# Gates of three sample tiles by accumulating indirect DMA instead of one-hot products, in a two-layer PEER trunk

## The chip, the cores and the metric

One core of a Trainium2 chip runs the whole program in one launch. The metric is device time in microseconds, 4672.34 us as the median of three runs before the change (4671.4 to 4675.66). The engines are named as the profile names them: PE is TensorE, DVE is VectorE, ACT is ScalarE, POOL is GpSimd and SP is SyncE, whose queue issues most of the plain DMAs.

## The reference, cut to what matters

Two layers run over 640 tokens: 128 prompt tokens and 512 sample tokens. Each layer ends with a PEER mixer. For each token and each of 8 heads it picks 16 of 16,384 experts by product keys, forms softmax gates, and sums gated expert outputs:

```python
s1 = einsum('thd,hnd->thn', q[:, :, 0], k1); s2 = einsum('thd,hnd->thn', q[:, :, 1], k2)
v1, i1 = top_k(s1, 16); v2, i2 = top_k(s2, 16)
cand = v1[..., :, None] + v2[..., None, :]          # 256 candidates per token and head
sv, si = top_k(cand, 16); eidx = i1 * 128 + i2 at si
gates = softmax(sv)
act = gelu(einsum('phkd,pd->phk', u_tab[eidx], x))  # one dot per chosen expert
out = einsum('phk,phkd->pd', gates * act, v_tab[eidx])
```

## The kernel before, in words

The kernel is a series of stages, each a block with one instruction stream per engine, joined by semaphores. The first layer's mixer is a gated DeltaNet (`delta_stage`), the second's a Fourier stage. Both layers then run PEER in two stages, under the names p0u/p0v and p1u/p1v.

The first expert stage (`experts_in_stage`, p0u and p1u) treats the two groups of tokens differently.

- **Sample tokens** are computed densely. A loop of 128 blocks `b` multiplies all 16,384 rows of the table `u` with all 512 sample tokens; a block has 128 experts and 24 products (L624). SP loads the block (`p0uraw`), ACT rounds it (`split_hi`, L651), DVE takes the rest (`split_lo`, L767), PE multiplies, ACT applies the gelu (L693) and stores to `a_scratch`. Only the routed gates make this sparse: a dense array `g_scratch[i1, i2, token]` holds each sample token's gate at its chosen experts and zero elsewhere, and the second stage multiplies both arrays.
- **Prompt tokens** are computed sparsely. For each of 128 slots (8 heads times 16 picks) POOL gathers one row of `u` per token by indirect DMA into `ring` (L757), and DVE takes the dot with the token (L872).

The gates are found tile by tile, 128 tokens each. PE makes the scores (L637), and DVE routes a tile in 21 steps (`route`): top 16 per key half, candidates, top 16 again, picks, gates. `route_plan` spreads these steps over blocks. In the kernel before, the prompt tile is the first (scores in block 1), and the four sample tiles follow.

For a sample tile, `g_scratch` is built from one-hot products, in 32 "quads" of 4 tokens: DVE compares the two key numbers of each pick with an iota (L778), ACT makes gated one-hots (L661 to L673), PE multiplies both per token (L612), ACT copies the sums to `g` (L681), and half a tile is stored in four DMAs (L686). `quad_plan` gives each sample tile a window of 23 blocks from block 32 on, `dot_plan` puts the prompt dots into blocks 32 to 127. Each engine works strictly in the order of this code, so a DVE wait in block `b` holds every later `split_lo`, and through it PE.

The second expert stage (`experts_out_stage`) reads `g_scratch` and `a_scratch` and multiplies with the table `v`; POOL gathers the prompt rows of `v` there.

Of the kernel before, what the change touches and what calls it, by code (L numbers as in the profile page):

```python
# [21 lines left out]
F32 = mybir.dt.float32  # L22
# [455 lines left out]
NQUADS = NQ * DEC_TILES  # L478
HALF_QUADS = NQ // 2
HALF_TOK = P // 2  # L480
STORES = 4
WIN = 23
W0 = 32
SCORES = [1, 15] + [W0 + WIN * k for k in range(DEC_TILES - 1)]
WINDOWS = [W0 + WIN * k for k in range(DEC_TILES)]
PAIRS = P
RING = 3


def quad_plan():  # L490

    plan = [[] for _ in range(P)]
    for k, w in enumerate(WINDOWS):
        for q in range(NQ):
            plan[w + q * WIN // NQ].append(k * NQ + q)
    return plan


def route_plan(n_tasks):

    plan = [[] for _ in range(P)]
    for k, s in enumerate(SCORES):
        span = (12, 11)[k] if k < 2 else WIN - 6
        for i in range(n_tasks):
            plan[s + 2 + i * span // n_tasks].append((k, i))
    return plan


def dot_plan():

    plan, n = [[] for _ in range(P)], 0
    for b in range(W0, P):
        for _ in range(2 if b >= P - (PAIRS - (P - W0)) else 1):
            plan[b].append(n)
            n += 1
    assert n == PAIRS, n
    return plan


def experts_in_stage(nc, m, tag, d, l, hi, lo, q_dram, a_dram, g_dram, x_dram, eidx, ew, eg):  # L520
# [10 lines left out]
        sm(x) for x in ("h_turned", "h_taken", "listed", "dot_done", "gelu_done", "weighed"))  # L531
    table = d[f"urows{l}"]
    with ExitStack() as es:
# [21 lines left out]
        tops = sb("tops", [P, 2, 4, P])  # L555
        oh1, oh2 = sb("oh1", [P, 3, QUAD, P]), sb("oh2", [P, 3, QUAD, P])
        g = [sb(f"g{j}", [P, P, HALF_TOK]) for j in range(2)]
# [9 lines left out]
        def _(sp):  # L567
# [12 lines left out]
            def load_q(k):  # L580
                if k:
                    sp.wait_ge(scored, k)
                else:
                    sp.wait_ge(spilled, 16)
                sp.dma_start(qt, q_dram[:, :, k * P:(k + 1) * P].rearrange("h p t -> p h t")).then_inc(q_full, 16)
# [5 lines left out]
            for b in range(2, P):  # L591
                load(b)
                for k in range(1, DEC_TILES + 1):
                    if b == SCORES[k - 1] + 6:
                        load_q(k)
                    if b == SCORES[k] - (0 if k < 3 else 3):
                        load_keys(k)

        @block.tensor
        def _(pe):  # L600
# [14 lines left out]
            for b in range(P):  # L615
# [11 lines left out]
                for k in range(DEC_TILES + 1):  # L627
                    if b == SCORES[k]:
# [3 lines left out]
                        if k > 1:  # L632
                            pe.wait_ge(t_taken, 2 * (k - 1))
# [5 lines left out]
                    if k and b == WINDOWS[k - 1] - 4:  # L639
                        pe.wait_ge(ready, k + 1)  # L640
# [5 lines left out]
        def _(act):  # L646
# [6 lines left out]
            def distances(n):  # L653
                if n < NQUADS and n % 2 == 0:
# [5 lines left out]
                    for e in range(QUAD):  # L660
                        last = nc.scalar.activation(oh2[:, n % 3, e, :], iota, ACT.Abs, bias=tops[:, k % 2, 0, t0 + e:t0 + e + 1], scale=-1.0)  # L661
                    last.then_inc(far, 1)

            def gated_one_hots(n):
                if n < NQUADS:
                    k, t0 = n // NQ, n % NQ * QUAD
                    act.wait_ge((far, near)[n % 2], n // 2 + 1)
                    for e in range(QUAD):
                        x, gate_t, minus_t = oh2[:, n % 3, e, :], tops[:, k % 2, 2, t0 + e:t0 + e + 1], tops[:, k % 2, 3, t0 + e:t0 + e + 1]
# [6 lines left out]
            def take(n):  # L676
                h, t0 = n // HALF_QUADS, n % HALF_QUADS * QUAD
                if n % HALF_QUADS == 0 and h >= 2:
# [4 lines left out]
            def store_half(h, s):  # L683
                i0, t0 = s * (P // STORES), h * HALF_TOK
                act.wait_ge(taken, (h + 1) * HALF_QUADS)
                act.dma_start(g_dram[i0:i0 + P // STORES, :, t0:t0 + HALF_TOK].rearrange("i p t -> p i t"),  # L686
# [18 lines left out]
            halves_due = []  # L705
            for b in range(P + 1):
# [19 lines left out]
                for k in range(DEC_TILES):  # L726
                    if b == WINDOWS[k] - 3:
                        act.wait_ge(turned, k + 1)
                        nc.scalar.copy(tops[:, k % 2, 0:3, :], bank[2][:, 0:3, :]).then_inc(t_taken, 1)
                        nc.scalar.mul(tops[:, k % 2, 3, :], bank[2][:, 2, :], -1.0).then_inc(t_taken, 1)  # L730
# [4 lines left out]
                for h, s in halves_due[:1]:  # L735
                    store_half(h, s)
                del halves_due[:1]
                for n in quads[b]:
# [3 lines left out]
                    if n % HALF_QUADS == HALF_QUADS - 1:  # L742
                        halves_due += [(n // HALF_QUADS, s) for s in range(STORES)]
            assert not halves_due
# [4 lines left out]
            act.wait_ge(g_stored, 16 * STORES * 2 * DEC_TILES)  # L749

        @block.gpsimd
        def _(pool):
            pool.wait_ge(listed, 1)
            for n in range(PAIRS):
                if n >= RING:
                    pool.wait_ge(dot_done, n - RING + 1)
                nc.gpsimd.indirect_dma_start(out=ring[:, n % RING, :], out_offset=None, in_=table,  # L757
                                             in_offset=bass.IndirectOffsetOnAxis(ap=eidx[:, n:n + 1], axis=0)).then_inc(row_full[n % RING], 16)

        @block.vector  # L760
        def _(dve):
# [7 lines left out]
            def plain_one_hots(n):  # L769
                if n < NQUADS:  # L770
# [6 lines left out]
                    for oh, row, sem in rows_of:  # L777
                        v.tensor_tensor(oh[:, n % 3], iota.unsqueeze(1).to_broadcast([P, QUAD, P]),  # L778
                                        tops[:, k % 2, row, t0:t0 + QUAD].unsqueeze(2).to_broadcast([P, QUAD, P]), ALU.is_equal).then_inc(sem, 1)
# [46 lines left out]
            def gates(k):  # L826
# [3 lines left out]
                out = gate[:] if k else eg[:].rearrange("p (h k) -> p h k", h=PEER_HEADS)  # L830
                v.tensor_tensor(out, ex[:], rden[:].unsqueeze(2).to_broadcast([P, PEER_HEADS, TOPK]), ALU.mult).then_inc(ready, 1)
                if k == 0:
                    v.scalar_tensor_tensor(out=eidx[:], in0=rows[:, 0, :], scalar=float(P), in1=rows[:, 1, :],
                                           op0=ALU.mult, op1=ALU.add).then_inc(listed, 1)

            def route(k, i):
                if i == 0:
                    dve.wait_ge(s_taken, 4 * (k + 1))
                    if k > 1:
# [1179 lines left out]
```

## Time and profile before

| | us |
|---|---|
| median of three runs | 4672.34 (4671.4 to 4675.66) |
| the profiled execution | 4669.94 |
| its span, first to last instruction | 4668.2 |
| DeltaNet stage | 338.8 to 681.9 |
| first expert stage, layer 0 (p0u) | 1000.7 to 1896.9 |
| second expert stage, layer 0 (p0v) | 1907.7 to 2617.1 |
| first expert stage, layer 1 (p1u) | 3016.7 to 3905.2 |
| second expert stage, layer 1 (p1v) | 3916.4 to 4627.8 |

PE is busy for 92% of the span, DVE for 69%, ACT for 38%, POOL for 31%. The four expert stages are two thirds of the span. A matmul's end is modelled in the profile, so the length of a block is read from the starts of its products and not from the busy time.

### The profile page before, as it was taken

Reading aid. Unit: us, or ns where it says so; the run is one execution under the profiler, and the core shown is the slowest. Engines: PE = TensorE matmul, PEld = TensorE weight load, DVE = VectorE, ACT = ScalarE, POOL = GpSimd, SP = SyncE. Lnnn points to the kernel's source line nnn. Section 1 sums busy time; section 2 is a strip of 40 time slices with the busy share of each in tenths; the row PEclk is TensorE's granted clock in tenths of the full one; section 3 lists DMA queues with packets and bytes.
Section 4 is the critical chain, followed back from the end, with each engine's and each line's share of the span. In section 5 each row is a group of like instructions: output and inputs, shape, how many; then the busy total and the mean of one; then the engine's idle time right before and its main releaser. Section 6 shows DMA issues by size and latency. Waiting matters only on the chain. (4 is left out here: it accounts for less than half of the span.)

```text
span 4668.2 us, 58501 instructions
## 1 busy us (share of the span) xinstructions
PE 4298.8 (92%) x21997; PEld 3603.2 (77%) x21997; DVE 3216.9 (69%) x5003; ACT 1785.2 (38%) x3370; POOL 1436.3 (31%) x844
## 2 busy tenths in 40 slices
PE   6988888899999999899999877999999997999997
PEld 1988886687888877688888476888888776888885
DVE  3658863338779876688888623187897865888886
ACT  1330002223667666222222232235777663222222
POOL 1001100100112123566777301000121234777763
PEclk9999988999999999999999988999999998999998
DMA  5210002344587788988888502455787889888884
GB/s 206 69 37 5 1 37 72 144 160 153 193 257 238 228 278 279 327 287 293 289 292 287 208 29 85 149 170 166 239 251 233 266 289 310 295 291 287 294 287 168
DMA packets 566628, 951.23 MB, mean 204 GB/s; under 512 B 295264, under 2 KB 317024, under 8 KB 560992
## 3 DMA queue, kind: packets, MB, share of 16 engines
q1 hardware_dynamic: 188000, 534.59, 33.5%
q0 software_dynamic: 73728, 268.47, 16.0%
q10 hardware_dynamic: 304640, 144.73, 10.6%
q8 instruction: 160, 2.62, 0.2%
q14 instruction: 100, 0.82, 0.0%
HBM read 794.56 MB, written 153.09 MB: 203 GB/s over the span
## 5 line engine op out<-in xcount | busy, mean ns | idle before, releaser
L757 POOL DMA_INDIRECT p1uring<-in_urows,p1eidx x128 | 171.7, 1342 | 851.0 <-DVE p1ew L872 608.2
L757 POOL DMA_INDIRECT p0uring<-in_urows,p0eidx x128 | 166.5, 1300 | 862.6 <-DVE p0ew L872 621.3
L624 PE MATMUL p0ups<-hi,p0uwhi 128*128 128x512 f32 x1024 | 419.0, 409 | 12.4 <-DVE p0uwlo L767 12.4
L624 PE MATMUL p1ups<-hi,p1uwhi 128*128 128x512 f32 x1024 | 417.0, 407 | 11.3 <-DVE p1uwlo L767 11.3
L986 PE MATMUL p1vps<-p1vwhi,p1vvhi 128*128 128x512 f32 x1024 | 399.2, 390 | 23.6 <-DVE p1vwlo L950 23.6
L986 PE MATMUL p0vps<-p0vwhi,p0vvhi 128*128 128x512 f32 x1024 | 399.4, 390 | 20.3 <-DVE p0vwlo L950 20.3
L624 PE MATMUL p0ups<-lo,p0uwhi 128*128 128x512 f32 x1024 | 404.8, 395 | 0.0
L624 PE MATMUL p0ups<-hi,p0uwlo 128*128 128x512 f32 x1024 | 404.4, 395 | 0.0
L624 PE MATMUL p1ups<-lo,p1uwhi 128*128 128x512 f32 x1024 | 402.9, 393 | 0.0
L624 PE MATMUL p1ups<-hi,p1uwlo 128*128 128x512 f32 x1024 | 402.6, 393 | 0.0
L986 PE MATMUL p0vps<-p0vwhi,p0vvlo 128*128 128x512 f32 x1024 | 399.1, 390 | 0.0
L986 PE MATMUL p0vps<-p0vwlo,p0vvhi 128*128 128x512 f32 x1024 | 399.1, 390 | 0.0
L986 PE MATMUL p1vps<-p1vwlo,p1vvhi 128*128 128x512 f32 x1024 | 399.0, 390 | 0.0
L986 PE MATMUL p1vps<-p1vwhi,p1vvlo 128*128 128x512 f32 x1024 | 398.8, 389 | 0.0
L932 POOL TENSOR_TENSOR p0vvlo<-p0vraw,p0vvhi 128x1024 fp32r<-128x1024 f32 x128 | 339.1, 2649 | 194.1 <-ACT p0vvhi L918 194.0
L932 POOL TENSOR_TENSOR p1vvlo<-p1vraw,p1vvhi 128x1024 fp32r<-128x1024 f32 x128 | 336.7, 2630 | 199.5 <-ACT p1vvhi L918 199.4
L918 ACT CAST p1vvhi<-p1vraw 128x1024 fp32r<-128x1024 f32 x128 | 134.8, 1053 | 492.4 <-PE p1vps L986 485.7
L918 ACT CAST p0vvhi<-p0vraw 128x1024 fp32r<-128x1024 f32 x128 | 134.7, 1053 | 487.1 <-PE p0vps L986 476.4
L767 DVE TENSOR_TENSOR p0uwlo<-p0uraw,p0uwhi 128x1024 fp32r<-128x1024 f32 x128 | 156.5, 1222 | 212.3 <-ACT p0uwhi L651 211.5
L767 DVE TENSOR_TENSOR p1uwlo<-p1uraw,p1uwhi 128x1024 fp32r<-128x1024 f32 x128 | 156.5, 1222 | 202.3 <-ACT p1uwhi L651 201.6
L986 PEld LDWEIGHTS p1vps<-p1vwhi,p1vvhi 128*128 128x128 f32 x1024 | 192.6, 188 | 63.9 <-POOL p1vvlo L932 23.9
L986 PEld LDWEIGHTS p0vps<-p0vwhi,p0vvhi 128*128 128x128 f32 x1024 | 192.7, 188 | 61.0 <-issue 21.0
(464 smaller groups left out, 10928.6 us busy)
## 6 DMA issues: line engine op xcount, KB each, us to landing
p0uraw<-in_u SPq DMA_DIRECT2D x128, 512.0 KB, 4.2
p0vraw<-in_vrows SPq DMA_DIRECT2D x128, 512.0 KB, 3.9
p1uraw<-in_u SPq DMA_DIRECT2D x128, 512.0 KB, 4.2
p1vraw<-in_vrows SPq DMA_DIRECT2D x128, 512.0 KB, 3.8
slab<-in_ada_w SPq DMA_DIRECT2D x24, 2048.0 KB, 7.6
a_scratch<-p0ua_out ACTq DMA_DIRECT2D x128, 256.0 KB, 4.0
g_scratch<-p0ug ACTq DMA_DIRECT2D x32, 1024.0 KB, 9.6
p0vga<-g_scratch SPq DMA_DIRECT2D x128, 256.0 KB, 4.1
```

Of the source, the lines that this page charges most:

```text
L624: mm = nc.tensor.matmul(psums[b % 2][:], x[:, b % 3, c * P:(c + 1) * P], y[:, c, S_CTX:T], start=c == 0 and n == 0, stop=c == NC - 1 and n ...
L757: nc.gpsimd.indirect_dma_start(out=ring[:, n % RING, :], out_offset=None, in_=table, in_offset=bass.IndirectOffsetOnAxis(ap=eidx[:, n:n + ...
L767: v.tensor_tensor(wlo[:, b % 3, :], raw[:, b % 2, :], whi[:, b % 3, :].bitcast(F32), ALU.subtract).then_inc(lo_done, 1)
L918: nc.scalar.copy(vhi[:, s % 3, :], raw[:, s % 3, :]).then_inc(v_hi, 1)
L932: nc.gpsimd.tensor_tensor(vlo[:, s % 3, :], raw[:, s % 3, :], vhi[:, s % 3, :].bitcast(F32), ALU.subtract).then_inc(v_lo, 1)
L986: mm = nc.tensor.matmul(psums[c][:], x[:, s % 3, c * P:(c + 1) * P], y[:, s % 3, :], start=s == 0 and n == 0, stop=s == P - 1 and n == 2)
```

## The change

For the first three sample tiles the gates are no longer made by one-hot products. DVE computes for each pick the flat address of its cell in `g_scratch`, and POOL adds the gate there by an indirect DMA with an add: one DMA per slot, 128 single float32 elements, one per token. Two heads of a token may choose the same expert, so the 16 DMAs of a head are issued only when the head before it, of the same tile, has landed. `phase_plan` interleaves the heads of neighbouring tiles. The array must be zero beforehand: each layer has its own `g_scratch` now, and 32 DMAs from SP clear the 384 columns of the three tiles in both, in the DeltaNet stage, from a block of zeros that DVE sets. The fourth sample tile still goes by quads, over 44 blocks from block 76 on, stored in four parts of 32 tokens.

The order of the tiles becomes sample 0, 1, 2, prompt, sample 3, with scores 14 blocks apart (blocks 1, 15, 29, 43, 57) and 12 blocks of routing each. The prompt dots go to blocks 74 to 125, from a ring of 6 rows instead of 3. The second expert stage is unchanged.

```diff
-WIN = 23
-W0 = 32
-SCORES = [1, 15] + [W0 + WIN * k for k in range(DEC_TILES - 1)]
-WINDOWS = [W0 + WIN * k for k in range(DEC_TILES)]
-RING = 3
+PARTS = 4
+PART_TOK = P // PARTS
+ORDER = (1, 2, 3, 0, 4)
+SCATTERED = 3
+SCORES = [1 + 14 * r for r in range(TILES)]
+W0, WIN = 76, 44
+DOT0 = 74
+RING = 6
 def dot_plan():
...
+    for n in range(PAIRS):
+        plan[DOT0 + n * (P - 2 - DOT0) // PAIRS].append(n)
+def phase_plan():
+    H = PEER_HEADS // 2
+    plan = [(0, h) for h in range(H)]
+    for t in range(SCATTERED - 1):
+        for h in range(H):
+            plan += [(t, H + h), (t + 1, h)]
+    for h in range(H):
+        plan += [(SCATTERED - 1, H + h), (SCATTERED, 2 * h), (SCATTERED, 2 * h + 1)]
+    return plan
...
         def _(pool):
-            pool.wait_ge(listed, 1)
-            for n in range(PAIRS):
-                if n >= RING:
-                    pool.wait_ge(dot_done, n - RING + 1)
-                nc.gpsimd.indirect_dma_start(out=ring[:, n % RING, :], ...)
+            for t, h in phase_plan():
+                if t < SCATTERED:
+                    if h == 0:
+                        pool.wait_ge(scat_ready, 2 * (t + 1))
+                    else:
+                        pool.wait_ge(scattered[t], 16 * TOPK * h)
+                elif h == 0:
+                    pool.wait_ge(listed, 1)
+                for n in range(h * TOPK, (h + 1) * TOPK):
+                    if t < SCATTERED:
+                        nc.gpsimd.indirect_dma_start(out=cells, out_offset=bass.IndirectOffsetOnAxis(ap=gidx[:, t, n:n + 1], axis=0),
+                                                     in_=gval[:, t, n:n + 1], in_offset=None, compute_op=ALU.add).then_inc(scattered[t], 16)
+                    else:
+                        if n >= RING:
+                            pool.wait_ge(dot_done, n - RING + 1)
+                        nc.gpsimd.indirect_dma_start(out=ring[:, n % RING, :], ...)
+            for sem in scattered:
+                pool.wait_ge(sem, 16 * PAIRS)
...
             def gates(k):
+                if k < SCATTERED:
+                    st.link(v.scalar_tensor_tensor(out=flat_idx[:], in0=rows[:, 0, :], scalar=float(P), in1=rows[:, 1, :],
+                                                   op0=ALU.mult, op1=ALU.add))
+                    v.scalar_tensor_tensor(out=gidx[:, k, :], in0=flat_idx[:], scalar=float(S_DEC), in1=tokens[:, k, :],
+                                           op0=ALU.mult, op1=ALU.add).then_inc(scat_ready, 1)
...
 def delta_stage(...):
+    CLEAR = 8
+        zeros = sb("zeros", [P, CLEAR, SCATTERED * P])
         def _(sp):
+            sp.wait_ge(blank, 1)
+            for dst in g_dram:
+                for i in range(0, P, CLEAR):
+                    sp.dma_start(dst[i:i + CLEAR, :, 0:SCATTERED * P].rearrange("i p t -> p i t"), zeros[:]).then_inc(cleared, 16)
             sp.wait_ge(s_new, DH)
...
+            sp.wait_ge(cleared, 16 * DEPTH * P // CLEAR)
+            v.memset(zeros[:], 0.0).then_inc(blank, 1)
```

POOL's whole stream in the first expert stage of layer 0 is, before, one run of gathers of prompt rows:

```order
L757 DMA p0uring<-in_urows,p0eidx 128x1024 x128
```

And after, where `g_scratch<-p0ugval,p0ugidx` is the adding DMA of one slot (128 elements):

```order
L774 DMA g_scratch<-p0ugval,p0ugidx 8388608x1 x336
L779 DMA p0uring<-in_urows,p0eidx 128x1024 x32
L774 DMA g_scratch<-p0ugval,p0ugidx 8388608x1 x16
L779 DMA p0uring<-in_urows,p0eidx 128x1024 x32
L774 DMA g_scratch<-p0ugval,p0ugidx 8388608x1 x16
L779 DMA p0uring<-in_urows,p0eidx 128x1024 x32
L774 DMA g_scratch<-p0ugval,p0ugidx 8388608x1 x16
L779 DMA p0uring<-in_urows,p0eidx 128x1024 x32
```

So 336 adding DMAs stand ahead of the first gathered prompt row, and the other 48 among the 128 gathers.

DVE around its first dot of layer 0, before: `p0uwlo` is the split of a block, `p0uoh` a one-hot of a quad, `p0uring,p0ew` a dot (in two instructions):

```order
L831 TENSOR_TENSOR p0ugate<-p0uex,p0urden 128x128
L767 TENSOR_TENSOR p0uwlo<-p0uraw,p0uwhi 128x1024 x4
L778 TENSOR_TENSOR p0uoh<-mats,p0utops 128x512 x3
L767 TENSOR_TENSOR p0uwlo<-p0uraw,p0uwhi 128x1024
L778 TENSOR_TENSOR p0uoh<-mats,p0utops 128x512 x3
L872 ISA p0uring,p0ew<-p0uring,xT 128x1024
```

And after, in blocks 71 to 76, behind the last gates of the fifth tile:

```order
L856 TENSOR_TENSOR p0ugate<-p0uex,p0urden 128x128
L791 TENSOR_TENSOR p0uwlo<-p0uraw,p0uwhi 128x1024 x4
L909 ISA p0uring,p0ew<-p0uring,xT 128x1024
L909 ISA p0ew 128x1
L909 ISA p0uring,p0ew<-p0uring,xT 128x1024
L909 ISA p0ew 128x1
L909 ISA p0uring,p0ew<-p0uring,xT 128x1024
L909 ISA p0ew 128x1
L791 TENSOR_TENSOR p0uwlo<-p0uraw,p0uwhi 128x1024
L802 TENSOR_TENSOR p0uoh<-mats,p0utops 128x512 x3
```

The first dots have moved from block 32 to block 74, ahead of the first one-hots of the quads (block 75), and they come two or three to a block.

## Rows read from the trace of the kernel before

**Rows 1.** busy time by stage: DeltaNet, first expert stage of both layers

```profile
core 0: us, PE busy (x) PEld busy (x) DVE busy (x) ACT busy (x) POOL busy (x), PEclk, DMA share, GB/s
338.80:681.90 343.10, 294.46 (x2400) 284.83 (x2400) 273.61 (x467) 24.41 (x46) 52.06 (x40) 0.96 0.02 7
1000.70:1896.90 896.20, 855.94 (x4268) 722.73 (x4268) 687.23 (x1610) 537.66 (x1196) 166.46 (x128) 0.98 0.73 232
3016.70:3905.20 888.50, 851.53 (x4268) 720.17 (x4268) 686.63 (x1609) 538.52 (x1196) 171.74 (x128) 0.98 0.74 234
```

**Rows 2.** TensorE waits, expert stage of layer 0 (total, times, longest)

```profile
PE p0upair L612 <- DVE p0uoh L778: 18.4, 9, 4.4
PE p0ups L624 <- DVE p0uwlo L767: 12.4, 3, 6.6
```

**Rows 3.** nine blocks without quads, eight with eleven; quads alone

```profile
1018.03:1067.12 49.09, 49.09 (x220) 40.71 (x219) 40.37 (x171) 14.32 (x20) 0.00 (x0) 1.00 0.44 140
1228.20:1281.92 53.72, 53.72 (x281) 45.89 (x280) 52.78 (x171) 39.65 (x95) 11.76 (x7) 1.00 0.62 205
...
1228.20:1281.92 53.72, 11.58 (x88) 11.51 (x88) 6.27 (x11) 1.00 0.62 205
```

**Rows 4.** fourteen blocks of routing, first and second tile; the split

```profile
1009.10:1094.90 85.80, 82.95 (x369) 68.67 (x368) 70.48 (x219) 27.15 (x36) 0.00 (x0) 0.96 0.47 154
1094.90:1180.90 86.00, 82.24 (x371) 67.77 (x371) 71.40 (x226) 27.37 (x36) 3.06 (x3) 0.98 0.46 153
...
L767 DVE TENSOR_TENSOR p0uwlo<-p0uraw,p0uwhi 128x1024 fp32r<-128x1024 f32 x15 | 18.3, 1218 | 19.9 <-ACT p0uwhi L651 19.7
```

**Rows 5.** timeline, layer 0: list of prompt rows, first three gathers

```profile
1095.97 0.29 DVE L833 SCALAR_TENSOR_TENSOR p0eidx<-p0urows 128x128 uint32<-128x128 f32 x1
1096.54 1.11 POOL L757 DMA_INDIRECT p0uring<-in_urows,p0eidx  x1 [233.68 <-DVE p0eidx L833]
1096.93 1.23 DVE L767 TENSOR_TENSOR p0uwlo<-p0uraw,p0uwhi 128x1024 fp32r<-128x1024 f32 x1 [0.68 <-ACT p0uwhi L651]
1097.95 1.02 POOL L757 DMA_INDIRECT p0uring<-in_urows,p0eidx  x1 [0.30 <-issue]
1099.27 0.93 POOL L757 DMA_INDIRECT p0uring<-in_urows,p0eidx  x1 [0.30 <-issue]
```

**Rows 6.** timeline, layer 1: the same three gathers

```profile
3111.51 1.69 POOL L757 DMA_INDIRECT p1uring<-in_urows,p1eidx  x1 [234.19 <-DVE p1eidx L833]
3113.51 0.94 POOL L757 DMA_INDIRECT p1uring<-in_urows,p1eidx  x1 [0.30 <-issue]
3114.75 0.94 POOL L757 DMA_INDIRECT p1uring<-in_urows,p1eidx  x1 [0.30 <-issue]
```

**Rows 7.** gathers of the first expert stage: ns min/median/max, landing

```profile
L757 POOL DMA_INDIRECT p0uring<-in_urows,p0eidx x128: 932/982/1912, 1096.5 to 1890.9; - x128
DMA to landing us min/median/max: 4.1/6.2/10.9
```

**Rows 8.** timeline: a gather issued while VectorE's split runs

```profile
1292.97 1.22 DVE L767 TENSOR_TENSOR p0uwlo<-p0uraw,p0uwhi 128x1024 fp32r<-128x1024 f32 x1
1293.33 1.68 POOL L757 DMA_INDIRECT p0uring<-in_urows,p0eidx  x1 [5.28 <-DVE p0ew L872]
```

**Rows 9.** the last stretch of the stage, with two gathers a block

```profile
1712.70:1896.90 184.20, 169.25 (x834) 143.16 (x832) 110.47 (x164) 105.03 (x242) 57.57 (x48) 0.95 0.91 290
```

**Rows 10.** DMA queues and issues: KB each, median us to landing

```profile
q0 software_dynamic: 73728, 268.47, 16.0%
...
p0uraw<-in_u SPq DMA_DIRECT2D x128, 512.0 KB, 4.2
a_scratch<-p0ua_out ACTq DMA_DIRECT2D x128, 256.0 KB, 4.0
```

**Rows 11.** VectorE's dot of one gathered row per token

```profile
L872 DVE CUSTOM_DVE_ANT_0 p0uring<-p0uring,xT 128x1024 f32<-128x1024 f32 x128 | 154.3, 1218 | 14.8 <-DMA p0uring<-in_urows,p0eidx 13.6 <-DVE p0urest L811 0.6
```

**Rows 12.** clearing of o_acc at the start of the DeltaNet stage

```profile
L1682 DVE MEMSET o_acc<- 128x2560 f32 x1 | 2.2, 2192 | 0.5 <-issue 0.5
```

More of the change, by code:

```diff
@@ L501, in route_plan @@
     plan = [[] for _ in range(P)]
-    for k, s in enumerate(SCORES):
-        span = (12, 11)[k] if k < 2 else WIN - 6
+    for r, s in enumerate(SCORES):
         for i in range(n_tasks):
-            plan[s + 2 + i * span // n_tasks].append((k, i))
+            plan[s + 2 + i * 12 // n_tasks].append((r, i))
     return plan
 def dot_plan():
[L511 to L516, printed above, removed]
+    plan = [[] for _ in range(P)]
+    for n in range(PAIRS):
[9 more added lines that the diff above has]
+        plan += [(SCATTERED - 1, H + h), (SCATTERED, 2 * h), (SCATTERED, 2 * h + 1)]
     return plan
@@ L531, in experts_in_stage @@
         sm(x) for x in ("h_turned", "h_taken", "listed", "dot_done", "gelu_done", "weighed"))
+    pcol_ready, paired, scat_ready = sm("pcol_ready"), sm("paired"), sm("scat_ready")
+    scattered = [sm(f"scattered{t}") for t in range(SCATTERED)]
     table = d[f"urows{l}"]
@@ L554, in experts_in_stage @@
         den, rden = sb("den", [P, PEER_HEADS]), sb("rden", [P, PEER_HEADS])
-        tops = sb("tops", [P, 2, 4, P])
+        tops = sb("tops", [P, 4, P])
+        gidx, gval = sb("gidx", [P, SCATTERED, P], U32), sb("gval", [P, SCATTERED, P])
+        pcol, flat_idx, tokens = sb("pcol", [P, 1]), sb("flat_idx", [P, P]), sb("tokens", [P, SCATTERED, P])
         oh1, oh2 = sb("oh1", [P, 3, QUAD, P]), sb("oh2", [P, 3, QUAD, P])
-        g = [sb(f"g{j}", [P, P, HALF_TOK]) for j in range(2)]
+        g = [sb(f"g{j}", [P, P, PART_TOK]) for j in range(2)]
         ring = sb("ring", [P, RING, D])
@@ L595, in _ @@
                         load_q(k)
-                    if b == SCORES[k] - (0 if k < 3 else 3):
+                    if b == SCORES[k]:
                         load_keys(k)
@@ L660, in distances @@
                     for e in range(QUAD):
-                        last = nc.scalar.activation(oh2[:, n % 3, e, :], iota, ACT.Abs, bias=tops[:, k % 2, 0, t0 + e:t0 + e + 1], scale=-1.0)
+                        last = nc.scalar.activation(oh2[:, n % 3, e, :], iota, ACT.Abs, bias=tops[:, 0, t0 + e:t0 + e + 1], scale=-1.0)
                     last.then_inc(far, 1)
@@ L725, in _ @@
                     nc.scalar.activation(ex[:], ex[:], ACT.Exp).then_inc(exp_done, 1)
[L726 to L730, printed above, removed]
+                if b == W0 - 3:
+                    act.wait_ge(turned, 1)
+                    nc.scalar.copy(tops[:, 0:3, :], bank[2][:, 0:3, :]).then_inc(t_taken, 1)
+                    nc.scalar.mul(tops[:, 3, :], bank[2][:, 2, :], -1.0).then_inc(t_taken, 1)
                 if b == W0 - 1:
@@ L734, in _ @@
                     gated_one_hots(0)
-                for h, s in halves_due[:1]:
-                    store_half(h, s)
-                del halves_due[:1]
+                for h, s in parts_due[:1]:
+                    store_part(h, s)
+                del parts_due[:1]
                 for n in quads[b]:
@@ L741, in _ @@
                     take(n)
-                    if n % HALF_QUADS == HALF_QUADS - 1:
-                        halves_due += [(n // HALF_QUADS, s) for s in range(STORES)]
-            assert not halves_due
+                    if n % PART_QUADS == PART_QUADS - 1:
+                        parts_due += [(n // PART_QUADS, s) for s in range(STORES)]
+            assert not parts_due
             act.wait_ge(dot_done, PAIRS)
@@ L844, in route @@
                     candidates(k)
-                    if k == 1:
+                    if k == SCATTERED + 1:
                         dve.wait_ge(listed, 1)
@@ L857, in _ @@
             split_lo(1)
+            v.tensor_tensor_reduce(flat_idx[:], ident, iota, 1.0, 0.0, ALU.mult, ALU.add, pcol[:]).then_inc(pcol_ready, 1)
+            dve.wait_ge(pcol_ready, 1)
+            for t in range(SCATTERED):
+                st.done(v.tensor_scalar(tokens[:, t, :], m["ones"][:], pcol[:, 0:1], float(t * P), ALU.mult, ALU.add))
+            st.wait()
             for b in range(P):
@@ L1869, in build @@
         q_dram = nc.dram_tensor("q_scratch", [NSC, P, T], F32, kind="Internal").ap()
-        g_dram = nc.dram_tensor("g_scratch", [P, P, S_DEC], F32, kind="Internal").ap()
+        g_dram = [nc.dram_tensor(f"g_scratch{l}", [P, P, S_DEC], F32, kind="Internal").ap() for l in range(DEPTH)]
         a_dram = nc.dram_tensor("a_scratch", [P, P, S_DEC], F32, kind="Internal").ap()
```

69 lines of the change are left out of this document (35 added, 34 removed).

## The prediction

> **What bounds the kernel now.** I read the busy time by stage first, then what PE waited for in the first expert stage, then that stage block by block, and last POOL's gathers one by one.
>
> The reader is to see in [rows 1] that the first expert stage belongs to PE: it is busy 855.9 of 896.2 us in layer 0 and 851.5 of 888.5 in layer 1, DVE 687, ACT 538, POOL 166. PE's waits there are short, 18.4 us for one-hots and 12.4 us for splits [rows 2]. So its length is a sum of PE's instructions. Nine blocks without quads take 49.09 us, 5.45 each; eight blocks with eleven quads (88 products) take 53.72 us, so a quad costs (53.72 - 8 x 5.45) / 11 = 0.92 us of PE's time [rows 3]. Fourteen blocks with the scores and the routing of a tile take 85.9 us, 10 more than 14 x 5.45, for the score batch and waits: there DVE is busy 70.5 of 85.8 us and nearly sets the pace [rows 4].
>
> POOL is idle most of the time there, and this is what the change spends. What bounds the stage after it depends on how fast POOL issues 336 adding DMAs.
>
> **The change part by part.**
>
> *Quads removed.* 96 of 128 per layer: 96 x 0.92 = 88 us of PE in each. Of the 31 us of PE's waits that have a cause in [rows 2], the one-hots' 18 us mostly go too. If nothing new came up, a stage would end near 896 - 88 - 18 = 790 us.
>
> *Routing.* Five tiles at 14 blocks each, in the pace of the first two tiles of before: block 71 begins at 8.4 + 5 x 85.9 = 438 us after the stage's first product, block 76 at 438 + 5 x 5.45 = 465 us. The two more small DVE instructions of a scattered tile cost 0.29 us each, like the list of rows in [rows 5]: under 1 us a tile.
>
> *The new chain on POOL.* It begins when the first tile's gates and addresses are there. In the trace of before the first routed tile gives its list at 1096.26, which is 95.6 us after the stage's first product [rows 1, 5]. From then on POOL issues 336 adding DMAs before the first gather of prompt rows. DVE's first dot stands in block 74, at about 455 us; behind it are queued all later splits, and the one-hots that PE wants in block 76. So if the first row is late, PE stops at about 467 us.
>
> The trace shows no adding DMA. The nearest row is a gather with 128 row indices. Where POOL issues back to back its starts are 1.41 and 1.32 us apart in layer 0, 2.00 and 1.24 us in layer 1 [rows 5, 6]; the mean is 1.49 us. The lower end is 1.24 (0.94 busy, 0.30 of issue) with DVE idle; the upper 2.00, when DVE runs a split: a gather that starts 0.36 us into a split of 1.22 us takes 1.68 us instead of 0.94 [rows 7, 8]. Neither end holds for an add that costs POOL more or less than a gather; this is under the rivals. I take 1.49, since the four intervals lie beside running routing, as most of the 336 will.
>
> Each of the heads 1 to 4 of the first tile waits for the landing of the head before, with nothing else to issue. A gather of 0.5 MB lands 6.2 us after its start [rows 7], so a wait costs about 6.2 - 1.49 = 4.7 us, four of them 19 us. Later heads have another head's 16 DMAs between them, 24 us, more than the 10.9 us of the longest landing. The Trainium skill (DMA: Bandwidth & Descriptors, "Anatomy of one DMA") puts the fixed cost of such a DMA at about 2.0 us, mostly completion; by that estimate the four waits would be some 2 us in all and the sum 17 us smaller. No run here shows a small one, so the sum stays with the gather.
>
> The first prompt row is there at 95.6 + 336 x 1.49 + 19 + 6 = 621 us. PE stands from 467 to 621, 154 us, against 88 + 18 us saved.
>
> *The rest of the stage.* After 621 us there are 51 blocks and 31 quads for PE: 51 x 5.45 + 31 x 0.92 = 306 us. DVE has 51 splits and 128 dots of 1.22 us [rows 4, 11], 218 us and the one-hots; POOL has 176 DMAs of 1.49, 262 us. Both fit beside PE. The transfers fit less well: 128 gathers of 0.524 MB (268.47 MB in 512 gathers), 49 table blocks of 512 KB, 51 stores of 256 KB [rows 10], and four parts of the gates of 2.1 MB (128 x 128 x 32 x 4 bytes), in all 115 MB. The last stretch of the stage before, also with two gathers a block, moves 290 GB/s with the DMA engines 91% busy [rows 9]. At 290 GB/s, 115 MB take 396 us; at 290 / 0.91 = 319 GB/s, 360. So the rest lasts 306 us if PE sets it and 360 to 396 if the transfers do. I take the middle of 306 and 360, 333. The stage then ends at 621 + 333 = 954 us: 58 us later than before in layer 0, 65 in layer 1.
>
> *Cheap parts.* The zeros: a memset of 3072 columns, at 2192 ns for 2560 [rows 12], is 2.6 us on DVE at the start of the DeltaNet stage, on the path. The clearing itself is 50.3 MB, 174 us at 290 GB/s, beside a stage of 343 us that moves 7 GB/s and runs on PE and DVE [rows 1]; it costs nothing while it stays under 343 us, and if the short runs of 1536 bytes halved the rate it would cost 5. The smaller work of ACT (take, one-hots, stores) is off the path already.
>
> *A rule that speaks against the change.* The split delays the gather that starts inside it until it ends [rows 8]. In the other direction the trace shows nothing of the kind: a split that starts 0.39 us into a gather takes 1.23 us, against 1.22 [rows 4, 5]. The Trainium skill (SBUF — State Buffer, "Who interferes with whom") says that DVE instructions with two SBUF inputs and GpSimd instructions that read SBUF exclude each other, and that issue order decides who blocks. The first half agrees with 1.68 against 0.94 us; by the second half DVE would lose time to POOL as well while it routes. The sum would be the same by the one and by the other: PE waits for POOL at block 76 anyway, and a routing that is slower by less than 154 us disappears in that wait.
>
> *Sum.* 58 + 65 + 3 = 126 us on the profiled execution's 4669.9 (the span of 4668.2 and 1.7 around it), 4796; the median of the runs is 2.4 above that execution, so 4798.
>
> **The rivals.**
>
> *POOL is late, but little (faster).* Its DMAs come at the lower end, 1.24 us. The first row is there at 95.6 + 417 + 19 + 6 = 538 us, and the stage ends at 844 (306 more) to 871 (333): 25 to 52 us earlier in layer 0, 18 to 45 in layer 1, so 4575 to 4632, say 4600. For it: three of the four intervals are at or under 1.41, and from 467 us on DVE stands still and nothing holds POOL. Against it: the split alone is 18 of 86 us in the routing. The point that decides: 333 us before 892, the mean length of the stage, is 559 us, which is 1.30 us per DMA.
>
> *POOL is not late (faster).* The first row by block 74 or 76, 465 us, wants 344 us for 336 DMAs, 1.03 each. Then the stage ends at 465 + 306 to 465 + 333, and the program at about 4440 to 4490. For it: 4 bytes per index and not 4096. Against it: 1.03 is under every interval of the trace, and 0.30 of it is issue.
>
> *The add costs POOL twice a gather (slower still).* It has to read and write its target, so if each index needs twice the descriptors, 2 x 0.94 + 0.30 = 2.18 us: first row at 853, the stage ends at 1186, +290 and +297 us, 5260. At the 2.00 us of the slow gather it is 1125, and 5140.
>
> That the change does not do what it says would show as gathers at 95 us in POOL's stream; the order of the instructions excludes it.
>
> **How the numbers follow.** My forecast (1.31 to 1.75 us per DMA, first row at 560 to 709 us, time 4680 to 4970, likeliest 4798) gets 0.40; POOL little late 0.24; not late 0.10; twice the cost 0.20; and 0.06 is left for transfers that take the full 396 us or adds that hold the DMA engines. A measurement of this kernel can tell about 0.2% from no change, 9 us. Faster is 0.24 + 0.10 = 0.34; no change 0.06, from the edge of the forecast at 1.30 us; slower the rest, 0.60. The range runs from 4500, under the little-late case, to 5150, the slow gather's price: it leaves out the case without lateness and the upper half of the last.
>
> **What the profile after would show.** POOL's adding DMAs back to back from about 96 us into each first expert stage, with a mean distance that I give as 1.49 us; the first gather at 595 to 620 us; DVE's first dot waiting for `p0uring`, with PE idle about 150 us in block 76; then blocks of 6.1 us or more, with DMA share over 0.9. The removed quads would show as 256 products of L612's kind per layer instead of 1024. The forecast is wrong if the distance is under 1.3 us, or if PE goes through block 76 without a long wait; the rest is wrong if the blocks after the wait run at PE's own 5.45 us and 0.92 per quad.

## The result, and the profile after

The changed kernel takes 5221.17 us, median of 4 runs (5214.98 to 5223.72); the kernel before, beside it, 4671.87 (4669.01 to 4675.66). The ratio is 1.117, 95% interval 1.115 to 1.119: 549 us slower. The forecast was slower by 126 us; 5221 lies above its range.

The profiled execution has a span of 5221.7 us against 4668.2. Busy time by stretch shows where the 553.5 us are; the columns are those of [rows 1], the stretches in turn the DeltaNet stage, the first expert stage of layer 0, its middle, its blocks 77 to 127, and the first expert stage of layer 1:

```profile
338.00:685.00 347.00, 295.06 (x2391) 285.75 (x2390) 274.85 (x459) 25.87 (x49) 52.07 (x40) 0.95 0.43 152
1008.40:2179.40 1171.00, 775.87 (x3491) 641.96 (x3491) 603.75 (x1478) 302.52 (x518) 817.70 (x512) 0.83 0.61 158
1465.00:1792.00 327.00, 1.78 (x8) 1.13 (x7) 3.96 (x7) 2.71 (x6) 270.51 (x177) 0.51 0.24 8
1801.40:2179.30 377.90, 323.85 (x1473) 267.72 (x1471) 225.47 (x335) 150.04 (x307) 241.31 (x165) 0.92 0.91 289
3296.50:4468.80 1172.30, 771.38 (x3491) 639.35 (x3491) 604.06 (x1479) 303.07 (x518) 820.17 (x512) 0.83 0.61 158
```

Against [rows 1] the two expert stages are 274.8 and 283.8 us longer. Before them 7.7 us were lost: the first window begins at 1008.4 us and not at 1000.7. What lies between and behind them takes 12.8 us less, and with this the sum is 553.5 (7.7 + 274.8 + 283.8 - 12.8); why it takes less was not tested. PE has 80 us less to do in each (775.87 for 855.94), and the stage is longer all the same: in the third row there are 327 us in which PE, DVE and ACT do next to nothing and POOL is busy for 270.5. The DMA engines are 24% busy there.

The waits of the same stage (engine, line, what it waited for, total, times, longest), of PE, of DVE, and of POOL:

```profile
PE p0upair L625 <- DVE p0uoh L802: 326.8, 1, 326.8
...
DVE p0uring L909 <- DMA p0uring<-in_urows,p0eidx: 404.9, 25, 329.9
...
POOL g_scratch L774 <- DMA g_scratch<-p0ugval,p0ugidx: 14.5, 6, 3.6
```

This is the predicted chain. PE waits for a one-hot, DVE for the first prompt row, and POOL, which is to fetch that row, still issues adds. In the wait the clock that PE is granted falls to 0.50, the lower of its two levels (1.2 GHz):

```profile
1500.00:1792.00 292.00, 0.00 (x0) 0.00 (x0) 3.96 (x7) 0.00 (x0) 241.09 (x158) 0.50 0.24 9
...
1796.00:1800.00 4.00, 4.00 (x12) 3.14 (x11) 4.00 (x7) 0.23 (x1) 3.12 (x2) 0.57 0.99 367
1800.00:1804.00 4.00, 4.00 (x23) 3.42 (x23) 2.98 (x5) 2.37 (x5) 3.23 (x3) 1.00 1.01 385
```

PE starts again at 1793.5 us, and from 1800 on the clock is at 1.00. An estimate from these rows is 3 us lost, half of the 6 us at the lower level, so the clock is not what makes the stage long. The durations of the adds and of the gathers (columns as in [rows 7]: ns min/median/max):

```profile
L774 POOL DMA_INDIRECT g_scratch<-p0ugval,p0ugidx x384: 1540/1547/3627, 1104.3 to 2082.3; - x192
...
L779 POOL DMA_INDIRECT p0uring<-in_urows,p0eidx x128: 933/1418/1988, 1782.8 to 2151.6; - x128
```

And POOL's timeline: the first adds, a change of heads, and the step from adds to gathers:

```profile
1104.29 2.43 POOL L774 DMA_INDIRECT g_scratch<-p0ugval,p0ugidx  x1 [234.47 <-DVE p0ugidx L864]
1107.03 1.58 POOL L774 DMA_INDIRECT g_scratch<-p0ugval,p0ugidx  x1 [0.31 <-issue]
...
1135.33 1.55 POOL L774 DMA_INDIRECT g_scratch<-p0ugval,p0ugidx  x1 [0.30 <-issue]
1139.14 1.55 POOL L774 DMA_INDIRECT g_scratch<-p0ugval,p0ugidx  x1 [2.27 <-DMA g_scratch<-p0ugval,p0ugidx]
...
1780.90 1.55 POOL L774 DMA_INDIRECT g_scratch<-p0ugval,p0ugidx  x1 [0.30 <-issue]
1782.75 0.99 POOL L779 DMA_INDIRECT p0uring<-in_urows,p0eidx  x1 [0.30 <-issue]
1784.05 0.96 POOL L779 DMA_INDIRECT p0uring<-in_urows,p0eidx  x1 [0.30 <-issue]
```

An add keeps POOL for 1.55 us, a gather that follows it at once for 0.96 to 0.99. From the first add to the first gather lie 678.5 us (1104.29 to 1782.75), 2.02 for each of the 336 adds. They are made of 336 x 1.547 = 520 us busy, 0.30 of issue each (100 us), the changes of heads (15 us), and about 42 us by which 41 adds are longer than the others. All 41 start while DVE has an instruction with two inputs under way, as this timeline of the two engines shows:

```profile
1144.70 1.55 POOL L774 DMA_INDIRECT g_scratch<-p0ugval,p0ugidx  x1 [0.30 <-issue]
1145.37 2.29 DVE L827 TENSOR_TENSOR p0ucand<-p0uval 128x2048 f32<-128x2048 f32 x1
1146.55 2.53 POOL L774 DMA_INDIRECT g_scratch<-p0ugval,p0ugidx  x1 [0.30 <-issue]
1147.69 1.22 DVE L791 TENSOR_TENSOR p0uwlo<-p0uraw,p0uwhi 128x1024 fp32r<-128x1024 f32 x1
```

The add at 1144.70 has its usual length; the one that starts 1.18 us into DVE's instruction takes 0.98 us more. The split that starts inside this longer add keeps its 1.22 us. Nor do the 1.55 us come from a queue that has filled, as far as the trace shows: the second add of the stage (1107.03) takes 1.58 us already, and in the long wait the DMA engines are 24% busy.

The last 48 adds stand in runs of 16 among the gathers. Two timelines, of POOL and then of DVE, at the first run:

```profile
1849.25 1.68 POOL L779 DMA_INDIRECT p0uring<-in_urows,p0eidx  x1 [3.12 <-DVE p0ew L909]
1851.23 1.60 POOL L774 DMA_INDIRECT g_scratch<-p0ugval,p0ugidx  x1 [0.30 <-issue]
...
1880.75 1.54 POOL L774 DMA_INDIRECT g_scratch<-p0ugval,p0ugidx  x1 [0.30 <-issue]
1882.60 1.00 POOL L779 DMA_INDIRECT p0uring<-in_urows,p0eidx  x1 [0.31 <-issue]
```
```profile
1886.86 1.23 DVE L909 CUSTOM_DVE_ANT_0 p0uring<-p0uring,xT 128x1024 f32<-128x1024 f32 x1 [20.82 <-DMA p0uring<-in_urows,p0eidx]
```

Sixteen adds hold the next gather back by 31 us; the six rows in the ring are used up before, and DVE, with the splits queued behind its dot, stands for 20.8 us.

### The profile page after: what moved, and what is told of

Read it like the earlier page. It is cut to its first block and busy times, and to the rows that moved or that the text cites. A ratio compares the mean times of both kernels' runs of the same rounds, so it can differ in the third digit from the quotient of the medians.

```text
span 5221.7 us, 54323 instructions
## 1 busy us (share of the span) xinstructions
PE 4143.1 (79%) x20443; PEld 3444.3 (66%) x20443; DVE 3075.0 (59%) x4738; ACT 1315.4 (25%) x2014; POOL 2790.5 (53%) x1612
## 5 line engine op out<-in xcount | busy, mean ns | idle before, releaser
L774 POOL DMA_INDIRECT g_scratch<-p1ugval,p1ugidx x384 | 644.3, 1678 | 365.3 <-DVE p1ugidx L864 234.6
L774 POOL DMA_INDIRECT g_scratch<-p0ugval,p0ugidx x384 | 643.4, 1675 | 365.6 <-DVE p0ugidx L864 234.5
L969 POOL TENSOR_TENSOR p0vvlo<-p0vraw,p0vvhi 128x1024 fp32r<-128x1024 f32 x128 | 356.5, 2785 | 188.5 <-ACT p0vvhi L955 188.5
L969 POOL TENSOR_TENSOR p1vvlo<-p1vraw,p1vvhi 128x1024 fp32r<-128x1024 f32 x128 | 360.4, 2816 | 180.5 <-ACT p1vvhi L955 180.5
L909 DVE CUSTOM_DVE_ANT_0 p1uring<-p1uring,xT 128x1024 f32<-128x1024 f32 x128 | 152.7, 1221 | 410.0 <-DMA p1uring<-in_urows,p1eidx 409.9
L909 DVE CUSTOM_DVE_ANT_0 p0uring<-p0uring,xT 128x1024 f32<-128x1024 f32 x128 | 152.7, 1222 | 405.2 <-DMA p0uring<-in_urows,p0eidx 404.9
L625 PE MATMUL p1upair<-p1uoh 128*128 128x128 f32 x256 | 37.6, 294 | 343.0 <-DVE p1uoh L802 331.1
L980 DVE TENSOR_TENSOR p0vw<-p0vga 128x512 f32<-128x512 f32 x128 | 299.8, 2342 | 11.9 <-DMA p0vga<-a_scratch 11.9
L625 PE MATMUL p0upair<-p0uoh 128*128 128x128 f32 x256 | 36.0, 286 | 340.2 <-DVE p0uoh L802 326.8
L980 DVE TENSOR_TENSOR p1vw<-p1vga 128x512 f32<-128x512 f32 x128 | 280.2, 2189 | 11.1 <-DMA p1vga<-a_scratch 11.1
```

The source lines that it names most:

```text
L625: mm = nc.tensor.matmul(pairs_ps[n % 2][:, :, e], oh1[:, n % 3, e, :], oh2[:, n % 3, e, :], start=True, stop=True)
L774: nc.gpsimd.indirect_dma_start(out=cells, out_offset=bass.IndirectOffsetOnAxis(ap=gidx[:, t, n:n + 1], axis=0), in_=gval[:, t, n:n + 1], i ...
L909: v.tensor_tensor_reduce(ring[:, n % RING, :], ring[:, n % RING, :], hrow, 1.0, 0.0, ALU.mult, ALU.add, ew[:, n:n + 1]).then_inc(dot_done, 1)
L969: nc.gpsimd.tensor_tensor(vlo[:, s % 3, :], raw[:, s % 3, :], vhi[:, s % 3, :].bitcast(F32), ALU.subtract).then_inc(v_lo, 1)
L980: v.tensor_tensor(w[:, s % 3, :], ga[:, s % 3, 0, :], ga[:, s % 3, 1, :], ALU.mult).then_inc(w_ready, 1)
```

## The experiments

Where a kernel was run once, its time is one run beside 4667.69 us of the kernel before; those that were run several times have an interval. plain, half, plain_half, noadd and spread are edits of the changed kernel, parts_ring is one of the kernel before. The five others rebuild the stage for any split of the tiles; the lines shown of them are set against the changed kernel, and the blocks of scores, routing and quads, which go with the split, are left out.

**What an add costs: plain, half, plain_half.** plain drops the add from the indirect DMA (a repeated cell then keeps one gate only):

```diff
-    in_=gval[:, t, n:n + 1], in_offset=None, compute_op=ALU.add).then_inc(scattered[t], 16)
+    in_=gval[:, t, n:n + 1], in_offset=None).then_inc(scattered[t], 16)
```

> The 384 DMAs of a layer write their 128 elements without adding (a cell that two heads choose keeps one gate; the rest of the output is as before). Theory A (an add costs POOL more than a gather because of the add: it has to read its target as well, the index count is the same): POOL is busy 0.94 us per DMA with VectorE idle instead of 1.55, 1.24 us apart instead of 1.85; the 336 take 336 x (2.02 - 0.61) = 474 us, the first gather comes some 205 us earlier than 775, at 570 us of the stage, TensorE waits about 120 us in block 76 instead of 327, and the program takes 5221 - 2 x 205 = 4810 us. Rival B (writing single 4-byte cells of DRAM is what costs POOL, with or without the add): busy stays 1.55 us and the program 5220.

half keeps the add and sends 64 elements (half of the gates are left out):

```diff
-nc.gpsimd.indirect_dma_start(out=cells, out_offset=bass.IndirectOffsetOnAxis(ap=gidx[:, t, n:n + 1], axis=0),
-                             in_=gval[:, t, n:n + 1], in_offset=None, compute_op=ALU.add).then_inc(scattered[t], 16)
+nc.gpsimd.indirect_dma_start(out=cells, out_offset=bass.IndirectOffsetOnAxis(ap=gidx[0:P // 2, t, n:n + 1], axis=0),
+                             in_=gval[0:P // 2, t, n:n + 1], in_offset=None, compute_op=ALU.add).then_inc(scattered[t], 16)
```

> Each adding DMA covers 64 tokens instead of 128 (the gates of the other half of each scattered tile stay zero); the number of DMAs is the same. If POOL's time goes by the elements: a gather of 128 indices is 0.94 and an add 1.55, so an add of 64 should be near 0.5 x 1.55 = 0.78 plus a fixed part, 0.8 to 1.1 us, the first gather at 96 + 336 x 1.3 = 530 us and the program 4740 to 4850. If it is a fixed price of an adding DMA: 1.55 us as before and 5220.

plain_half makes both edits:

> A plain write of 64 elements in place of an add of 128 (the adding and half of the tokens' gates are left out). Measured so far: add of 128 busy 1.55 us, add of 64 1.41, plain write of 128 0.96. Theory (the add's surcharge of 0.59 us is a fixed price per DMA, an element costs 2.3 ns in either kind): busy about 0.81 us, interval about 1.11, time about 4660 to 4730 us. Rival (the surcharge is made of elements too, and the plain write's price is all fixed): busy about 0.95 us, and the time of the plain write of 128, 4783 us.

Measured: 4783.59, 5097.53 and 4730.51 us (beside 4670.31 for the last). The adds' line in each, in this order:

```profile
L774 POOL DMA_INDIRECT g_scratch<-p0ugval,p0ugidx x384: 952/958/2961, 1099.4 to 1861.5; - x192
```
```profile
L774 POOL DMA_INDIRECT g_scratch<-p0ugval,p0ugidx x384: 1402/1411/3470, 1101.3 to 2018.4; - x192
```
```profile
L774 POOL DMA_INDIRECT g_scratch<-p0ugval,p0ugidx x384: 886/892/2886, 1099.6 to 1827.5; - x192
```

A plain write costs POOL 0.96 us, what a gather costs [rows 7]; the add puts 0.59 us on it. With plain writes the first gather comes 584 us after the stage's first product, the writes are 1.45 us apart, and the kernel takes 4784: the forecast's sum, 1.49 us per DMA and 4798, would have fitted a write without the add. Half of the elements saves 0.14 us with the add and 0.07 without. So an element costs 2.1 ns (0.136 / 64) or 1.0 (0.066 / 64), and of the 0.59 us 0.52 remain at 64 elements; drawn on in a straight line to no elements, an estimate is that some 0.45 us are a price of the DMA. My expectation for half, 0.8 to 1.1 us, was wrong: fewer elements hardly help. plain_half lay between its two theories, 0.89 us where 0.81 and 0.95 were expected: that the surcharge is mostly a fixed price holds, that an element costs the same with and without the add doesn't.

**What POOL's lateness costs: noadd.** It leaves the adds and the wait for them out; the gates of three tiles stay zero, and the rows come when the list is there.

```diff
                 if t < SCATTERED:
+                    continue
...
-            for sem in scattered:
-                pool.wait_ge(sem, 16 * PAIRS)
```

> The adding DMAs are left out (the gates of three sample tiles stay zero); POOL issues only the 128 gathers of a layer. Theory A (the whole loss is POOL's time for 384 adds): no wait of TensorE in block 76, blocks 77 to 127 at 306 to 345 us instead of 378, a stage of 465 + 306 to 345 = 770 to 810 us, the program 5221 - 2 x (1171 - 790) = 4460 to 4540. Rival C (the transfers set the blocks after 76, 115 MB at 290 to 319 GB/s, whatever POOL does): blocks 77 to 127 stay at 360 to 380 us, a stage of 835 us, the program 4550. Before is 4672.

Measured: 4472.7 us, and the stage of layer 0 with its blocks 77 to 127:

```profile
1002.70:1806.00 803.30, 764.69 (x3491) 635.06 (x3491) 602.74 (x1478) 300.79 (x518) 175.64 (x128) 0.97 0.69 231
1466.00:1806.00 340.00, 315.61 (x1473) 262.86 (x1471) 224.38 (x335) 148.55 (x307) 159.92 (x117) 0.96 0.97 320
```

Without the adds the stage is 93 us shorter than before and PE has no long wait, so the whole loss is POOL's. The adds cost 749 us (5221 - 4473). The kernel without them is 195 us under the one before, and of these 18 belong to the ring and the smaller parts (parts_ring, below); the 192 quads that are gone make the other 177 at 0.92 us each. The last 51 blocks are not at PE's pace: 320 GB/s, the DMA engines 97% busy.

**The runs of sixteen: spread.** The last 48 adds are issued one by one between the gathers.

```diff
+            for n in range(PAIRS):
+                head.append((SCATTERED, n))
+                if n % 8 in (2, 5, 7):
+                    head.append(tail.pop(0))
```

> The last 48 adds of a layer stand one by one among the gathers (3 after every 8) instead of in three runs of 16; same work. Theory A (a run of 16 adds holds POOL for 31 us while the ring of 6 rows lasts VectorE 15 us): VectorE's three waits of 15 to 22 us for a row go, and with them some 34 us of TensorE's waits in blocks 89 to 115; blocks 77 to 127 take about 345 us instead of 378, the program 5221 - 2 x 33 = 5155. Rival C (the transfers set this part): unchanged, 5220.

Measured: 5155.13 us. Its blocks 77 to 127:

```profile
1795.90:2141.60 345.70, 320.27 (x1473) 265.94 (x1471) 227.49 (x337) 148.68 (x307) 247.91 (x165) 0.96 1.00 319
```

They take 345.7 us instead of 377.9, near noadd's 340.0. The runs cost 32 us in a layer. The DMA share is 1.00 then.

**Is it only the order: three_even, two_tiles.** Both put a prompt tile second, so that its rows are fetched from block 32 on, one or two a block, with the adds one by one between the gathers in an order that is worked out ahead from assumed costs. Three tiles go by adds in the one and two in the other; the other tiles by quads.

```diff
+KINDS = ['s', 'p', 's', 's', 'q']   # three_even
+KINDS = ['s', 'p', 's', 'q', 'q']   # two_tiles
-DOT0 = 74
+DOT0 = 32
...
+        if n < PAIRS and free <= t:
+            stream.append(("row", n))
+            t, n = t + 1.6, n + 1
+        elif adds and max(adds[0][0], last.get(adds[0][1:], 0.0)) <= t:
+            _, r, m = adds.pop(0)
+            stream.append((r, m))
+            t += 2.05
```

> Three tiles by adds as in the change, but with the prompt routed second and the adds one by one among the gathers, so that TensorE doesn't wait for rows in the middle; only the end of the stage waits for the adds. Theory A (POOL's throughput is the bound, wherever the wait stands): POOL's sum 96 + 384 x 1.85 to 2.05 + 128 x 1.45 to 1.6 = 990 to 1090 us is the length of the stage, against 1171 in the change and 892 before: the program 4672 + 2 x (100 to 200) = 4870 to 5070. Rival E (the order of rows and adds was the whole fault): a stage of 760 to 800 us, 4450 to 4500.

> Two sample tiles by adds, prompt routed second, dots evenly over blocks 32 to 125, adds one by one among the gathers. POOL: 96 us until the first gates, then 256 x 1.9 to 2.05 + 128 x 1.45 to 1.6, which ends at 770 to 850 us; TensorE's own sum is 128 x 5.45 + 64 x 0.92 + 18 = 775 us and some waits. Theory A: a stage of 800 to 860 us against 892, the program 4672 - 2 x 60 + 6 = 4560 (4490 to 4610). Rival D: 4660 or more.

Measured: three_even 5202.1 us, ratio 1.114 (1.112 to 1.116); two_tiles 4667.61, ratio 0.9994 (0.9985 to 1.0004). Of three_even, layer 0: the stage up to PE's last product, the stretch behind it, and what DVE waited for there:

```profile
1003.50:1812.80 809.30, 769.65 (x3491) 635.45 (x3491) 604.01 (x1478) 303.57 (x518) 542.09 (x330) 0.97 0.79 229
1812.80:2185.50 372.70, 0.00 (x0) 0.00 (x0) 5.89 (x4) 5.10 (x7) 287.85 (x186) 0.50 0.23 11
```
```profile
DVE p0vw L1013 <- DMA p0vga<-a_scratch: 365.5, 2, 364.4
```

PE goes through without the long wait and is done at 809 us, but the adds end at 1166 us, and the next stage, which reads the sums, starts 373 us after PE's last product. The wait has moved from block 76 to the end of the stage, and 19 us of 549 are gained: 512 DMAs of POOL with 824 us busy and 0.30 of issue each make 978 us from the first add on, whatever their order; 93 us of waits come on top, 53 for free rows and 40 at the changes of heads, more than my estimate of 990 to 1090 had room for, so the time lies above the 4870 to 5070 that I expected. In blocks 77 to 127 PE needs 307 us, the 306 that I had worked out; 64 gathers fall into them, where noadd has 117 and takes 340 us.

In two_tiles the products end at 816.5 us and the adds at 886.0; the same wait of DVE is

```profile
DVE p0vw L1013 <- DMA p0vga<-a_scratch: 81.9, 2, 81.6
```

What PE gains is lost there again. The time that I expected, 4490 to 4610, is missed. The number fits my rival, that adds cost the other engines time (4660 or more), but its reason does not: PE's part lies within my 800 to 860 us, and the median of a split is 1.224 us, as in the kernel before. What is late is POOL.

**More adds ahead of each gather: two_tight, two_tighter.** two_tiles with cheaper adds and gathers in the table (1.95 and 1.4 us, then 1.8 and 1.25), with 0.5, then 0.6 us more for a block with routing; this changes the order alone:

> Two tiles by adds, as in two_tiles, but the table of POOL's order is made with cheaper adds and gathers (1.95 and 1.4 us in place of 2.05 and 1.6), so that more adds stand ahead of each gather. In two_tiles POOL ended 65 us after TensorE's last product, with 110 us of waits at gathers whose buffer's row had not been dotted yet. Theory (those waits are made by the order, POOL itself would be done with about 96 + 256 x 1.9 + 128 x 1.4 = 761 us of work): POOL's last add at 820 to 860 us after the stage's first product instead of 886 to 892, the next stage 30 to 70 us earlier per layer, 4530 to 4610 us. Rival (POOL can't go faster, because its adds wait for VectorE's splits): the stage ends as in two_tiles, 4640 to 4680 us.

> As two_tight, with 1.8 and 1.25 us in the table of the order: still more adds ahead of each gather. Theory: POOL's last add another 0 to 25 us earlier, but the gathers now lag behind VectorE, so that TensorE waits in the blocks with dots and its own part of the stage gets longer than 820 us; 4510 to 4610 us, on either side of two_tight. Rival (POOL can't go faster): 4640 to 4680 us, with POOL's waits gone and its instructions longer.

Measured: two_tight 4608.25 us, ratio 0.987 (0.985 to 0.989); two_tighter 4710.24, ratio 1.008 (1.007 to 1.010). POOL's waits for a free row, in two_tiles and in two_tight, layer 0:

```profile
POOL p0uring L800 <- DVE p0ew L942: 31.1, 20, 5.0
```
```profile
POOL p0uring L800 <- DVE p0ew L942: 1.8, 6, 0.3
```

The waits in two_tiles are 31 us and not the 110 that my expectation names. In two_tight they are nearly gone, and its adds end 28 us earlier (858.3 for 886.0), within the 820 to 860 expected; but rows come later now (DVE waits 139.8 us for them in layer 0), and PE's part of the stage grows from 816.5 to 847.2 us. In two_tighter it grows to 922.6, and the adds end at 854.3; its time lies above both theories. So with two tiles POOL is done near 860 us at best, and the 761 us of work that I had reckoned had the adds too cheap: among the gathers of two_tight they are busy for 1.81 us in the mean and not 1.60 (1.90 with the issue). The order still decides 100 us of the program, since rows that come late hold PE.

**One tile by adds: one_tile.** The prompt tile first, one sample tile by adds, three by quads.

```diff
+KINDS = ['p', 's', 'q', 'q', 'q']
```

> The kernel before with its order of tiles (prompt first, dots from block 32), where only the first sample tile goes by adds: 128 adds per layer from block 29 on, one by one among the gathers; three tiles by quads; gates in parts of 32 tokens, ring of 6. Theory A (POOL's time is the only price, and it fits here: 128 x 2.0 + 128 x 1.6 = 460 us of a stage of 860): each layer gains 32 quads x 0.92 = 29 us and up to 6 us of waits, minus 5 us of clearing in all: 4672 - 60 to 70 + 5 = 4605 to 4620. Rival D (adds cost the other engines time as well, by the shared port or the DMA engines): VectorE's splits and one-hots get longer, and it is 4660 or more.

Measured: 4588.1 us (4586.27 to 4588.55), ratio 0.982 (0.981 to 0.984). The stage in both layers, and POOL's longest sum of waits in layer 0 once it has the list of rows:

```profile
1005.40:1857.80 852.40, 825.45 (x4009) 691.55 (x4009) 659.53 (x1568) 461.94 (x969) 400.94 (x256) 0.98 0.85 237
...
2973.00:3831.20 858.20, 828.51 (x4009) 694.39 (x4009) 659.54 (x1568) 462.38 (x970) 403.22 (x256) 0.97 0.85 235
```
```profile
POOL p0uring L803 <- DVE p0ew L945: 182.7, 43, 10.5
```

PE is busy for 97% of the stage again, and POOL waits for DVE, not the other way round. It beats both kernels. The rival that adds slow the other engines is out: a split has its 1.224 us here too. My 4605 to 4620 is missed by 17 us, which the next run accounts for.

**The ring and the smaller parts alone: parts_ring.** The kernel before with a ring of 6 and gates stored in four parts, and no add:

```diff
+PARTS = 4
+HALF_QUADS = NQ // PARTS
...
-RING = 3
+RING = 6
```

> The kernel before, with gates stored in parts of 32 tokens instead of 64 and a ring of 6 rows instead of 3, no adds: the control for the three above. Expected: 4672 within 0.3% (4658 to 4686) if neither matters; the stores' runs of 128 bytes instead of 256 are twice the packets, which may cost some us in the last 40 blocks where the DMA engines are 91% busy, and the longer ring may give some back.

Measured: 4653.56 us, ratio 0.996 (0.995 to 0.998). They are worth 18 us by themselves, under the 4658 that I gave as the edge of no effect; which of the two it is was not tested. So the one tile by adds is worth some 65 us beyond them (4653.6 - 4588.1), where the 64 quads that it removes (32 in each layer) make 59 at 0.92 us each.

## Why the prediction was wrong

The direction and the mechanism were right: POOL's 336 adds ahead of the first prompt row hold PE in block 76. The step that failed is the price of one add. I took 1.49 us, the mean distance of four gathers beside running routing, and it is 2.02. Point by point, layer 0:

| step | predicted | measured |
|---|---|---|
| stage without POOL's lateness | 790 us | 803 (noadd) |
| first add after the stage's first product | 95.6 | 95.9 |
| PE reaches block 76 | 465 | 457 |
| distance of two adds | 1.49 | 2.02 |
| first gather issued | 615 | 774.4 |
| PE's wait in block 76 | 154 | 327 |
| blocks from 77 on | 333 | 378 |
| stage | 954 | 1171 |

Of the 217 us that are missing in the stage, 159 come from the distance of the adds: 336 x (2.02 - 1.49) = 178, less the 19 us of head waits that I had counted apart and that are part of the 2.02. From the blocks behind the wait come 45. The other 13 lie between the first gather and block 77, 18.6 us where the sum had 6 for the landing alone: the landing takes 4.5, three dots, a split and the one-hots on DVE 6.3, and block 76 the rest, in part at the lower clock.

*The price of an add.* The range for it, 1.24 to 2.00 us, was drawn from gathers only, an undisturbed and a disturbed one, and both have a gather's own 0.94 us in them. With nothing in its way an add takes 1.85 us (1.55 and 0.30), near the upper end, and interference comes on top. The right reading of [rows 5 to 8] would have been that they bound what happens around an indirect DMA and say nothing of an add inside it. The rival "twice a gather" (2.18 us, 5260) was the nearest case and had 0.20. Its reason was half right: the surcharge is for the add, but 0.59 us and mostly per DMA, not another 0.94. The range stopped at 5150, under that rival.

*The blocks behind the wait.* I took 333 us, the middle between PE's 306 and the transfers' 360. The transfers fit as the bound: 340 us without adds, 346 with adds spread (DMA share 0.97 and 1.00, 320 and 319 GB/s), and 307 in three_even, where half of the gathers lie elsewhere. That it is the transfers and not the dots on DVE, which go with the gathers, was not tested apart. 319 GB/s from [rows 9] was right; the 360 was too long because the stretch moves 109 MB (340 us at 320 GB/s) and not 115. What I didn't price are the runs of sixteen adds, 32 us by spread: they are longer than a ring of six rows lasts. PE's 306 and its prices per block and per quad held (307 in three_even).

*Head waits.* Four waits of 4.7 us, 19 in all, were forecast; there are six, 14.5 us, 1.7 to 3.6 each, and the four that I had in mind make 11.1. I had taken the landing of a gather of 0.5 MB for one of 512 bytes. The Trainium skill (DMA: Bandwidth & Descriptors, "Anatomy of one DMA") puts the fixed part at about 2.0 us, and by that estimate the four would have been 2 us. The trace lies between, and neither price decides anything here.

*The rule that spoke against the change.* Adds do get longer beside two-input instructions of DVE (2.53 us for 1.55), as gathers did. DVE's splits are not slowed in turn: of the 75 between the first product of layer 0's stage and the long wait, 46 start inside an add, and none of them takes more than 1.23 us; the median of all is 1.224 us here and 1.225 in noadd. Of what the Trainium skill states (SBUF — State Buffer, "Who interferes with whom"), that a DVE instruction with two SBUF inputs and a GpSimd instruction that reads SBUF exclude each other and that issue order decides who blocks, this case shows the one direction only.

*Cheap parts.* The memset of the zeros takes 2.62 us, as forecast. From its first copy to the next stage's first product the DeltaNet stage takes 4.7 us more than before (348.9 for 344.3), but nothing more in noadd, which has the same stage (344.0); the clearing, with the DMA engines 43% busy there, stayed hidden. The expert stage's first product comes 7.4 us later here and 1.4 us (spread) to 4.4 us (half) later in kernels that are the same up to there, so a good part of it differs from one execution to the next. Routing kept its pace. noadd's stage is 93 us shorter than before where I had 106 for the quads and their waits, and parts_ring puts 9 of a layer on the ring and the parts. The 4575 of the rival with little lateness lacks the 3 us of the zeros.

## What to carry to other kernels

An idle engine's time is spent by the price of one of its instructions times their number: before 336 of a kind are put ahead of something on the path, one of that kind has to be measured, since the nearest row of another kind bounds only what lies around it. Where work moves to a side engine, its whole sum must end before the consumer. If it doesn't, a better order moves the lateness to another wait (three_even); if it nearly does, the order decides (two_tiles and two_tight). So move as much as fits (one tile here, 1.8% faster than the kernel before, 1.4% of it by the adds) and not as much as can be expressed. A ring of buffers should outlast the longest run of other work between two of its loads: here sixteen adds outlasted six rows and cost 32 us.

## What was not expected of the hardware

An indirect DMA with an add keeps POOL for 1.55 us against 0.96 for the same write without it, with 128 elements of 4 bytes each; with 64 elements it is 1.41 against 0.89. From 128 elements to 64 the price falls by a tenth or less, and a write of single cells costs as much as a gather of whole rows of 4 KB (0.94 to 0.98).
